# Softmax attention with the values as TensorE's weights, and a reordered start of the latent attention

## What is computed

```python
qa, ka, va, fa, qc, kc, vc, gates = jnp.split(rms_norm(x, norm1) @ w_in, SPLITS, axis=-1)
# forgetting attention: causal, c = cumsum of log(sigmoid(fa + forget_bias))
p = softmax(where(key <= query, qa @ ka.T * scale + c[query] - c[key], NEG));  o_a = p @ va
# chunk-band attention: key's chunk of 64 no later than the query's, a learned bias by distance
p = softmax(where(valid, qc @ kc.T * scale + rel_bias[clip(query - key)], NEG)); o_b = p @ vc
```

```python
cq, ckv, k_pe = split(x @ w_in)                      # 768, 256, 32 columns
q = rms_norm(cq) @ w_q_b                             # per head 64 + 32 (rotary) columns
k_nope, v = split(rms_norm(ckv) @ w_kv_b)            # per head 64 and 64
q_pe, k_pe = apply_rope(q_pe), apply_rope(k_pe)      # pairs of columns turned by the position's angle
s = (q_nope @ k_nope.T + q_pe @ k_pe.T) * scale      # masked by chunks of 64 positions
o = softmax(s) @ v
```

## Time and profile before

| | |
|---|---|
| device time, 3 runs | median 2447.7 us (2447.54 to 2453.76) |
| the profiled execution | 2452.62 us, its span 2450.8 us |
| granted TensorE clock, mean | 0.976 |
| PE busy | 2319.1 us, 95% of the span, 14110 instructions |
| PEld busy | 1910.0 us, 78% |
| DVE busy | 1025.8 us, 42% |
| ACT busy | 881.1 us, 36% |
| POOL busy | 248.9 us, 10% |

### The profile page before, as it was taken

One profiled execution on the slowest core, in us unless ns is written; L12 is line 12 of the kernel. 1 busy time (PEld: TensorE's weight loads), 2 busy tenths in 40 slices (PEclk: granted clock), 3 DMA queues, 4 the chain that ended last, 5 costly groups with the idle time before them and its releaser, 6 DMA issues. The chain is left out here.

```text
span 2450.8 us, 34249 instructions
## 1 busy us (share of the span) xinstructions
PE 2319.1 (95%) x14110; PEld 1910.0 (78%) x14110; DVE 1025.8 (42%) x1494; ACT 881.1 (36%) x1540; POOL 248.9 (10%) x332
## 2 busy tenths in 40 slices
PE   5999999999999999969997999999989989999997
PEld 5887777888888887738886888888867769888886
DVE  2333215463344345437646543333533345333333
ACT  4444335242232244234322422222445554222223
POOL 3100000010000011013321300000420104000001
PEclk8999999999999999979998999999999999999998
DMA  3412113233333223200002233333332122333320
GB/s 109 117 52 53 43 26 112 81 101 90 97 93 91 79 82 90 62 0 1 0 2 82 85 99 92 95 95 95 74 80 50 35 61 62 103 103 101 96 87 35
DMA packets 346426, 178.41 MB, mean 73 GB/s; under 512 B 43878, under 2 KB 339988, under 8 KB 346284
## 3 DMA queue, kind: packets, MB, share of 16 engines
q1 hardware_dynamic: 344252, 171.54, 24.9%
q0 software_dynamic: 2032, 4.85, 0.7%
HBM read 171.35 MB, written 2.11 MB: 71 GB/s over the span
## 5 line engine op out<-in xcount | busy, mean ns | idle before, releaser
L500 PE MATMUL bank<-act_hi,w_hi 128*128 128x512 f32 (+1 forms) x1528 | 571.3, 374 | 21.0 <-DVE act_lo L830 8.1
L483 DVE TENSOR_TENSOR w_lo<-w,w_hi 128x1024 fp32r<-128x1024 f32 (+2 forms) x328 | 400.5, 1224 | 444.4 <-ACT w_hi L476 444.1
L502 PE MATMUL bank<-act_hi,w_lo 128*128 128x512 f32 (+1 forms) x1528 | 558.3, 365 | 0.0
L501 PE MATMUL bank<-act_lo,w_hi 128*128 128x512 f32 (+1 forms) x1528 | 556.9, 364 | 0.0
L476 ACT ACTIVATE w_hi<-w 128x1024 fp32r<-128x1024 f32 (+2 forms) x328 | 336.5, 1029 | 377.0 <-PE bank L502 258.6
L500 PEld LDWEIGHTS bank<-act_hi,w_hi 128*128 128x128 f32 x1528 | 292.0, 191 | 72.7 <-DVE w_lo L483 12.6
L502 PEld LDWEIGHTS bank<-act_hi,w_lo 128*128 128x128 f32 x1528 | 291.2, 191 | 48.7
L501 PEld LDWEIGHTS bank<-act_lo,w_hi 128*128 128x128 f32 x1528 | 292.4, 191 | 44.7
L500 PE MATMUL bank<-hid_hi,w_hi 128*128 128x512 f32 (+1 forms) x560 | 207.9, 371 | 0.0
L502 PE MATMUL bank<-hid_hi,w_lo 128*128 128x512 f32 (+1 forms) x560 | 207.2, 370 | 0.0
L501 PE MATMUL bank<-hid_lo,w_hi 128*128 128x512 f32 (+1 forms) x560 | 206.6, 369 | 0.0
(11 more groups left out here) (422 smaller groups left out, 3157.5 us busy)
## 6 DMA issues: line engine op xcount, KB each, us to landing
w<-in_ffn_w_gate_up SPq DMA_DIRECT2D x88, 512.0 KB, 3.8
w<-in_w_in SPq DMA_DIRECT2D x41, 512.0 KB, 3.9
w<-in_w_up SPq DMA_DIRECT2D x32, 512.0 KB, 4.0
w<-in_w_down SPq DMA_DIRECT2D x32, 512.0 KB, 3.7
w<-in_ffn_w_down SPq DMA_DIRECT2D x32, 512.0 KB, 3.6
w<-in_even_w_in SPq DMA_DIRECT2D x28, 512.0 KB, 3.9
w<-in_ffn_w_down SPq DMA_DIRECT2D x16, 384.0 KB, 3.0
w<-in_w_out SPq DMA_DIRECT2D x8, 512.0 KB, 3.7
```

Of the source, the lines that this page charges most:

```text
L483: e.tensor_tensor(w_lo[:, 0:part.n], w.raw[part.g % w.LOADS][:, 0:part.n], w_hi[:, 0:part.n].bitcast(F32), ALU.subtract).then_inc(w.lo.sem, 1)
L500: e.matmul(s.acc, *first, start=(k == 0), stop=False)
L501: e.matmul(s.acc, *second, start=False, stop=False)
L502: last = e.matmul(s.acc, *third, start=False, stop=(k == kt - 1))
```

## The change

**First block.** Both attentions become a `PairAttention`. Units of two heads alternate (head 2r, block 0; head 2r + 1, block 0; head 2r, block 1; ...). The values are the weights now (64 columns), and the transposed probabilities move (128 columns); the output comes out with features on the partitions, the even head in rows 0 to 63, the odd in rows 64 to 127 of one bank, so there are no transposes of the output and no division of it. Instead VectorE takes a unit's reciprocal and scales its probabilities before they are turned. The values products of a pair of units are issued together, heads in turn. For the banded attention (`apart=True`) the scores of a pair are issued together too. The transposed probabilities have a third buffer and their PSUM bank a second, and the output bank is copied once for two heads.

```diff
+class PairAttention(Hook):
+    SCALE, TURN, VALUES, OUT = 1, 2, 3, 4
...
+    def unit(n):
+        return n // 8 * 2 + n % 2, n // 2 % 4, (n // 2 % 4 + 1) * P
...
+    def scores(self, e, n, units):
+        for m in range(n, n + units):
+            self.ready(e, m)
+            if m >= 2:
+                e.wait_ge(*self.exped.at(m - 1))
+        for m in range(n, n + units):
+            head, i, keys = self.unit(m)
+            e.matmul(self.score[m % 2][:, 0:keys], self.queries(head)[:, P * i:P * i + P], self.keys(head)[:, 0:keys],
+                     start=True, stop=False)
+        for m in range(n, n + units):
+            head, i, keys = self.unit(m)
+            self.bias(e, self.score[m % 2], head, keys).then_inc(self.scored.sem, 1)
+    def turn(self, e, n):
+        i = self.unit(n)[1]
+        e.wait_ge(*self.scaled.at(n + 1))
+        if n >= 2:
+            e.wait_ge(*self.ready_p.at(n - 1))
...
+    def multiply(self, e, n):
...
+        e.wait_ge(*self.ready_p.at(n + 1))
...
+        for kt in range(i + 1):
+            for j in range(2):
+                last = e.matmul(self.o_bank[r % 2][HD * j:HD * j + HD, i * P:(i + 1) * P], self.values(kt, 2 * r + j),
+                                self.probs_T[:, (n - 1 + j) % 3, kt * P:(kt + 1) * P], start=(kt == 0), stop=(kt == i))
...
+    def vector(self, e, a, b):
+        for m in self.steps_in(a, b):
+            if m < self.UNITS:
...
+                e.tensor_reduce(self.neg_max[:, m % 4:m % 4 + 1], self.score[m % 2][:, 0:self.unit(m)[2]], AX.X, ALU.max,
+                                negate=True).then_inc(self.maxed.sem, 1)
+            if 0 <= m - self.SCALE < self.UNITS:
+                self.scale(e, m - self.SCALE)
...
+    def scale(self, e, n):
+        keys, inverse = self.unit(n)[2], self.inverse[:, n % 4:n % 4 + 1]
+        e.wait_ge(*self.exped.at(n + 1))
+        e.reciprocal(inverse, self.sums[:, n % 4:n % 4 + 1]).then_inc(self.inverted.sem, 1)
+        e.wait_ge(*self.inverted.at(n + 1))
+        e.tensor_scalar(self.probs[:, n % 3, 0:keys], self.probs[:, n % 3, 0:keys], inverse, None, ALU.mult)\
+         .then_inc(self.scaled.sem, 1)
```

```diff
     def gpsimd(self, e):
...
+        self.place(e, 0)
+        self.swap(e, 1)
+        x, places, placed = self.again
+        for rows, dst in places:
+            e.dma_start(dst, x[rows, :]).then_inc(placed.sem, 16)
+        self.place(e, 1)
+        for n in range(2, len(self.tiles)):
+            self.swap(e, n)
+            self.turn(e, n)
+            self.place(e, n)
...
+class RopeFirst(Hook):
...
+    def gpsimd(self, e):
+        self.rope.swap(e, 0)
...
-    names = ffn.names + ["kv", "k_pe", "q", "v0", "v1"] + [f"{s}{quad}" for quad in range(4) for s in ("kn", "qr", "qn")]
-    g = Gemm(core, ctx, [J[name] for name in names], norms=("up00", "kv"), first_parts=1, few_banks=J["kn1"], bank=bank)
+    names = ffn.names + ["kv", "k_pe", "q"]
+    names += [f"{s}{quad}" for quad in range(4) for s in (("v",) if quad < 2 else ()) + ("kn", "qr", "qn")]
+    g = Gemm(core, ctx, [J[name] for name in names], norms=("up00", "kv"), first_parts=1, few_banks=J["v1"], bank=bank)
...
-        places += places_over(span, 16)
+        places += places_over(span, 16, 1.4)
...
-    g.run(ffn.lead, ffn.first_norm, ffn.second_norm, kv_norm, q_norm, rope, mla)
+    g.run(ffn.lead, ffn.first_norm, ffn.second_norm, kv_norm, RopeFirst(rope), q_norm, rope, mla)
```

More of the change, by code:

```diff
@@ L1467, in add, with add_again, wait_again, swap @@
         return n
+    def add_again(self, x, places):
+        self.again = x, places, Span(self.core.sig("rope_again"), 16 * len(places))
     def wait(self, e, n):
         e.wait_ge(*self.tiles[n][6][2].at(16 * len(self.tiles[n][4])))
+    def wait_again(self, e):
+        e.wait_ge(*self.again[2].at(16 * len(self.again[1])))
+    def swap(self, e, n):
+        x, swapped, there, _, _, _, (swaps, _, _) = self.tiles[n]
+        e.wait_ge(*there)
+        for two in range(2):
+            e.dma_start(swapped[two:P:2, :], x[1 - two:P:2, :]).then_inc(swaps.sem, 16)
+    def place(self, e, n):
+        x, _, _, _, places, _, (_, turned, placed) = self.tiles[n]
+        e.wait_ge(*turned.at(3))
+        for rows, dst in places:
+            e.dma_start(dst, x[rows, :]).then_inc(placed.sem, 16)
+    def turn(self, e, n):
+        x, swapped, _, _, _, _, (swaps, turned, _) = self.tiles[n]
+        e.wait_ge(*self.table.at(2))
+        e.wait_ge(*swaps.at(32))
+        e.tensor_tensor(swapped, swapped, self.sine[:, :], ALU.mult).then_inc(turned.sem, 1)
+        e.tensor_tensor(x, x, self.cosine[:, :], ALU.mult).then_inc(turned.sem, 1)
+        e.wait_ge(*turned.at(2))
+        e.tensor_tensor(x, x, swapped, ALU.add).then_inc(turned.sem, 1)
     def gpsimd_first(self, e):
@@ L1481, in gpsimd @@
     def gpsimd(self, e):
-        for x, swapped, there, _, places, _, (swaps, turned, placed) in self.tiles:
-            e.wait_ge(*there)
-            for two in range(2):
-                e.dma_start(swapped[two:P:2, :], x[1 - two:P:2, :]).then_inc(swaps.sem, 16)
-            e.wait_ge(*turned.at(3))
-            for rows, dst in places:
-                e.dma_start(dst, x[rows, :]).then_inc(placed.sem, 16)
+        self.place(e, 0)
+        self.swap(e, 1)
+        x, places, placed = self.again
+        for rows, dst in places:
+            e.dma_start(dst, x[rows, :]).then_inc(placed.sem, 16)
+        self.place(e, 1)
[3 more added lines that the diff above has]
+            self.place(e, n)
     def vector_after(self, e, n):
@@ L2615, in plan @@
             add("q", 6, KD, columns(odd, 0, KD))
[L2616 to L2618 removed]
             for quad in range(4):
+                if quad < 2:
+                    jobs[f"v{quad}"] = TokenJob(w, f"v{quad}", 2, lambda k, n=quad: [
+                        (i, 1, 0, T, kv_b[:, i, 8 * n:8 * n + 8, HD:2 * HD]) for i in range(2)])
                 add(f"kn{quad}", 2, 2, heads(kv_b, 2, 2 * quad, 0, HD, 2), group=2)
```

96 lines of the change are left out of this document (84 added, 12 removed).

## The result

| | before | after |
|---|---|---|
| device time, first comparison, 4 executions each | 2450.05 us (2447.54 to 2453.76) | 2420.66 us (2419.94 to 2423.62) |
| all executions of this study | 2453.6 us (2444.56 to 2459.70, 36) | 2421.3 us (2418.95 to 2423.62, 12) |
| the profiled execution, its span | 2452.62, 2450.8 | 2423.62, 2421.8 |

The ratio of the first comparison is 0.9881, 95% interval 0.9863 to 0.9899: 29.4 us less by the medians. Forecast were 2418.1 us and 29.6 us less. The busy times, against the earlier trace rows: PE has 23.2 us less, VectorE (DVE) 14.1 more, POOL 14.9 more.

The account below looks back on a forecast made before the run. TensorE, busy 95% of the span, was taken to bound the kernel. First block -10, -15 and +6.1, odd layer -10.7: 29.6 us less than 2447.7, so 2418.1 us, own range 2414 to 2424, given range 2410 to 2435.

Parts of the forecast that it names:

- A: Values as weights in both first-block attentions, heads alternating, no output transposes: 10 us less; bounds 15 less to 7 more.
- B: Scores of two banded heads issued behind each other, fewer mode changes and the second score overlapped: 15 us less; bounds 4.8 and 15.
- C: First-block attentions: PE waits behind tile boundaries for VectorE's scaling and ScalarE's exponentials: 6 us more; bounds 0 and 15.
- D: Odd layer: shorter wait for placed rotary queries, no clock fall behind it, fewer query waits: 10.7 us less; bounds 5 and 13.
- Rival 1: Values bursts in the first block too short for the halves to overlap: 2444 us; chance 7%.
- Rivals 2: First-block waits behind tile boundaries two or three times as large, 12 to 18 us: 2424 to 2430 us; chance 14%.
- 3: Scaling paces every step, PE waiting at each of 64 units' transposes; at 0.8 us a unit 2463 us; chance 3%.
- 5: No waits behind tile boundaries and all of the odd layer's gain: 2410 to 2413 us; chance 9%.
- Behind a wait of 1.5 the clock should stay: Odd layer: with about 1.5 us of wait for placed queries left, clock stays at 2.4 GHz, 2.2 us less.
- The half about GpSimd: Odd layer: GpSimd's own turning of later queries is hidden, its swap issued over 20 us before PE asks.
- Rival 4: GpSimd's turning, nine products of 1.5 us, holds VectorE's weight splits; if all came to PE, 13 us: 2431 us; chance 2%.

Follow-up runs that it names:

- scores_alone: The changed kernel with the banded attention's scores issued one unit at a time instead of in pairs: 2436.1 us, ratio to before 0.9929.
- three_banks: The changed kernel with three banks for the banded scores and one for the turned probabilities: 2417.2 us, ratio to before 0.9858.
- the two variants above: The changed kernel with all eight key placements before the queries' swap (2428.5 us), or with the values' second half back before the first quad's keys (2421.2 us).
- odd_only: The changed kernel with the old Attention in the first block, so only the odd layer is changed: 2446.7 us, ratio to before 0.9974.
- keys_first: The changed kernel with all eight placements of the keys issued before the swap of the first quad's queries: 2428.5 us, ratio to before 0.9888.
- block_only: The kernel before with PairAttention in the first block, odd layer as before: 2436.4 us, ratio to before 0.9941.
- vector_turns: The changed kernel with VectorE instead of GpSimd turning the later quads' queries, as before: 2429.9 us, ratio to before 0.9900.
- values_serial: The changed kernel with all values products of the even head issued before those of the odd head in each burst: 2427.2 us, ratio to before 0.9903.
- latent_pairs: The changed kernel with the odd layer's attention also in the PairAttention form: 2420.9 us, ratio to before 0.9880.

## Why the prediction was right

**The numbers.** 2418.1 was forecast and 2420.7 measured, inside the 2410 to 2435, and faster by 29.4 us where 29.6 were forecast, clear of 0.3%. The agreement to 0.2 us is in part luck. Between the first two profiles A, B and C together gave 18.6 us where 18.9 were forecast, D 7.2 instead of 10.7, the recurrence 6.4 that no term has, and the rest of the program took some 3 back.

**A, right.** Eight alternating products take 1.02 us and two 0.37, as 0.22 i + 0.15 said. (The upper bound of 15 is misadded: at 0.15 a burst the working gives 16; nothing rests on it.) The causal stretch holds A's half and the causal part of C alone: -5 + 1.5 = -3.5, measured -3.2; all three waits for scaled probabilities, 1.3 us, lie in it, so A's half is 4.5. Rival 1, bursts too short to overlap, is out: with the heads not in turn 6.2 us are lost, and even that order overlaps in part. The transposes and the division that went were not tried apart from the products. The rule of the Trainium skill, "TensorEngine Tiling (Array Packing)", Theoretical Speedup, up to 2x for a dimension of 64 or less, agrees with the 0.11 against 0.22 for values and with the second head's scores, which are free (1.06 us for both).

**B, right.** 14.5 us by `scores_alone`, 15 forecast; the stretch fell by 15.4 where -5 - 15 + 4.6 = -15.4 was the sum. The 0.42 us of a pair of 128 columns fits the 0.2 behind the scores that B read from the earlier trace rows: 0.22 for both and 0.2. Key Properties of the same page of the Trainium skill has TensorE drained at a change of tiling mode, which speaks against short bursts. The 0.2 us over a product's own 0.22 agrees with it, though no run shows that a drain is what takes them; now two units share them.

**C, right.** 4.3 us in four waits on exponentials (4.6 forecast), 1.3 us in three on scaled probabilities, 0.9 the longest (1.5 forecast): 5.6 against 6.1, in seven waits where I had named about ten. Rivals 2, 3 and 5 are out, and `three_banks` shows the cause of the 4.3. Scaling takes 0.49 us for 512 columns and the reciprocal 0.16, 0.43 and 0.18 from the earlier trace rows:

```profile
L1450 DVE RECIPROCAL inverse_sums<-exp_sums 128x1 f32<-128x1 f32 x64 | 9.9, 155 | 4.1 <-ACT probs L1472 3.6
...
L1452 DVE TENSOR_SCALAR probs<-probs,inverse_sums 128x512 f32<-128x512 f32 x16 | 7.8, 487 | 0.6
```

**D, the wait right, the clock right behind it and wrong elsewhere.** By my times, 23.6 us earlier as all this stage now is, the placements would start at 1798.4, the swap at 1800.4 and be landed by 1805.7, PE would go at 1812.9; the trace has 1798.57, 1800.56, 1806.20 and 1813.72. The wait is 1.9 where 1.5 was forecast, and no fall follows it in any of the three profiles; behind 3.7 and 4.3 us, in the two variants above, it does. Two of the three waits of 1.53 us are gone, as forecast. What failed is to take "Behind a wait of 1.5 the clock should stay" for more than that place: behind the last quad's wait of 1.53 us it fell in two of the three profiles of the changed kernel, which takes back 4.7 of the 10.7 us. Of the ten profiles with the new odd layer and this wait four have the fall (these two, `odd_only`, `keys_first`), of the two with the old one (the kernel before, `block_only`) none; whether the new order makes it likelier is open. From `kv_hi` to the last values it is 7.2 us less than before in the first profile and 12.2 in the third, which has no fall. The half about GpSimd failed on the other side: that its turning "is hidden" is so, but it also takes the waits for exponentials away, 1.7 us of them in the kernel before and 3.5 in `vector_turns`, which no term of the sum had. Rival 4 didn't come: the products take 1.27 us on POOL and no wait of PE goes with them. But its premise is real, and the trace has its price elsewhere. None of the nine products met a weight split; all that VectorE did beside them were maxima, at their usual 0.69, 0.29 and 0.42 us. Where a norm's addition of 128x512 on GpSimd had begun just before a split of 128x1024, ten times in this profile, the split took 1.99 us instead of 1.22:

```profile
1990.42 1.29 POOL L1070 TENSOR_TENSOR norm_total<-norm_total,x 128x512 f32<-128x512 f32 x1 [4.15 <-DVE x L713]
1990.80 1.99 DVE L483 TENSOR_TENSOR w_lo<-w,w_hi 128x1024 fp32r<-128x1024 f32 x1 [0.46 <-ACT w_hi L476]
```

So rival 4 was missed by where the products happen to lie; nine such meetings would have held VectorE for nine times 0.77, 7 us (an estimate from these rows), and not 13.

**Not in the sum: the clock of the recurrence.** 6.4 us of the difference of the two profiles lie in a stage that the change doesn't touch. As it took 326.0 in the third profile, it isn't the change's, or not in each execution. Nor is it the chip's: each of the three groups has a profile with 320.7 to 321.2 and one with 326.5 or more. What the change would be worth at equal clocks can be read from executions at 0.979 or 0.980: seven of the kernel before, median 2446.3, and seven of the changed one, median 2420.3. That is 26.0 us, and rough: 0.001 of mean clock stands for 4.8 us at 1.2 GHz instead of 2.4, up to 2.4 us of time, and an equal mean doesn't say that the falls lie in the same stages. Why the changed kernel never met the 0.971 to 0.975 that 19 of the 32 executions of the kernel before in the three groups had, while each of the ten variants but `values_serial` met it at least once, is open; no run was made for it.

## What to carry to other kernels

A wait that is new on the bounding engine can be worked out ahead from the order of the queues and the durations around a tile's boundary. Where the steps were walked one by one, in C and D, such a sum came within a microsecond; where they weren't, in `latent_pairs`, 2 to 3 us were expected and 7.3 measured. Where a step writes 64 of the 128 output rows or reads 64, issue two heads' products next to each other: the second is nearly free, and a third bank of scores takes the waits away that pairing brings. A claim that an engine's work is hidden should be asked both ways: what it holds up where it stands now counts as well. A total that fits is no proof of its terms: here one term was 3.5 us too large and a stage that no term had gave 6.4.

## What the runs showed of the hardware

- Paired fp32 products of 64 rows (scores of two heads) took 1.06 us for 2 x 512 columns, as long as one head's in the earlier trace rows; products with 64 columns of weights in alternating halves 0.11 us each, and in blocks of four and four 1.51 us for eight, where without overlap it would be 1.91 (eight times 0.22 and 0.15).
- The same stage of the same kernel ran at another clock in another execution: recurrence 320.8 to 326.0 us, and the last quad with 10 us at 1.2 GHz or with none, behind the same wait of 1.53 us. The 36 executions of the kernel before spread over 15 us (2444.6 to 2459.7), the 32 whose mean clock is on record at 0.971 to 0.980, so of two parts of a change tried alone the medians (15.5 and 5.2) summed to 10 us less than the whole; only the stretches of the traces added up.
- Behind PE's waits of 1.1 to 2.0 us for the placed queries the clock stayed at 2.4 GHz in ten profiles, behind 3.7 and 4.3 us it fell to 1.2 GHz for 3.4 us, behind 7.0 and 7.9 us for longer (10.2 us, in part within the wait).
- GpSimd's product of 128x512 takes 1.27 us here, VectorE's 0.69. A weight split of 128x1024 on VectorE took 1.99 us instead of 1.22 where GpSimd had begun an addition of 128x512 just before it; VectorE's maxima, which read PSUM, took no longer beside GpSimd's products.
